# Feed-forward products of steps 3 to 10 written turned, the conditioning rows moved behind both down products, and three weight rests cut in halves

## The reference, cut to what matters

```
def swiglu(x, w_gate_up, w_down):
    g, u = jnp.split(x @ w_gate_up, 2, axis=-1)
    return (jax.nn.silu(g) * u) @ w_down
...
        x = layer_norm(ALPHA * x + mixed, ln1_g[i], ln1_b[i])
        x = layer_norm(ALPHA * x + swiglu(x, w_gate_up[i], w_down[i]), ln2_g[i], ln2_b[i])
...
def hybrid_layer(x, c_act, norm_g, w_ada, b_ada, w_in, w_out, pos):
    mod = c_act @ w_ada + b_ada
    shift, scale, gate = jnp.split(mod, 3, axis=-1)
    h = rms_norm(x, norm_g) * (1.0 + scale[:, None, :]) + shift[:, None, :]
```

## Time and profile before

| | |
|---|---|
| median of three runs | 1551.9 us |
| the profiled execution's own time | 1551.6 us |
| span of its trace | 1549.8 us |
| PE busy | 1527.2 us of the span (99%) |
| DVE busy | 1090.6 us (70%) |
| ACT busy | 759.4 us (49%) |
| mean granted clock of PE | 0.999 of full speed |

### The profile page before, as it was taken

One profiled execution on the slowest core, in us unless ns is written; L12 is line 12 of the kernel. 1 busy time (PEld: TensorE's weight loads), 2 busy tenths in 40 slices (PEclk: granted clock), 3 DMA queues, 4 the chain that ended last, 5 costly groups with the idle time before them and its releaser, 6 DMA issues.

```text
span 1549.8 us, 19849 instructions
## 1 busy us (share of the span) xinstructions
PE 1527.2 (99%) x8091; PEld 1267.2 (82%) x8091; DVE 1090.6 (70%) x1568; ACT 759.4 (49%) x960; POOL 52.8 (3%) x89
## 2 busy tenths in 40 slices
PE   9999999999999999999999999999999999999997
PEld 7887788888878888888788888877888888978986
DVE  6986866656787775677866757888667678567764
ACT  5657444444445443447544433566344434574463
POOL 1100000000000000000000000000100000000010
PEclk9999999999999999999999999999999999999999
DMA  8662566644435766353476654533766646433530
GB/s 323 243 227 83 207 221 263 250 172 181 163 109 193 262 260 250 136 215 112 158 258 226 245 233 143 197 109 137 272 253 240 222 164 224 164 119 140 218 123 27
DMA packets 45898, 299.87 MB, mean 193 GB/s; under 512 B 5540, under 2 KB 5796, under 8 KB 12528
## 3 DMA queue, kind: packets, MB, share of 16 engines
q1 hardware_dynamic: 39600, 278.74, 48.6%
q0 software_dynamic: 5776, 19.01, 3.7%
q10 hardware_dynamic: 432, 0.85, 0.1%
HBM read 296.20 MB, written 2.65 MB: 193 GB/s over the span
## 4 chain that ended last, share of the span: by engine, by line
PE 86%; DVE 8%; ACT 3%; issue 2%; DMA 0%; SPq 0%; POOL 0%; POOLq 0%; DVEq 0%; ACTq 0%
PE psum L1311 55%; PE psum L1270 15%; PE psum L1305 7%; DVE w_low L1779 2%; PE psum L1165 2%; PE psum L1240 1%; PE psum L1424 1%; PE psum L1327 1%; PE psum L1378 1%; PE psum L1308 1%; DVE work L2101 1%; ACT w_high L1530 1%; PE psum L1412 1%; DVE work L2063 1%; DVE w_low L1786 0%
## 5 line engine op out<-in xcount | busy, mean ns | idle before, releaser
L1530 ACT ACTIVATE w_high<-w_raw 128x2048 fp32r<-128x2048 f32 (+1 forms) x240 | 456.3, 1903 | 230.1 <-DMA w_raw<-in_weights 144.6
L1779 DVE TENSOR_TENSOR w_low<-w_raw,w_high 128x2048 fp32r<-128x2048 f32 (+2 forms) x240 | 526.0, 2196 | 40.2 <-ACT w_high L1530 39.2
L1311 PE MATMUL psum<-w_high,xt_high 128*128 128x512 f32 (+1 forms) x1376 | 378.6, 395 | 1.3 <-ACT xt_high L1539 1.3
L1311 PE MATMUL psum<-w_high,xt_low 128*128 128x512 f32 (+1 forms) x1376 | 368.4, 388 | 0.3 <-DVE xt_low L1813 0.3
L1311 PE MATMUL psum<-w_low,xt_high 128*128 128x512 f32 (+1 forms) x1376 | 368.1, 388 | 0.0
L1311 PEld LDWEIGHTS psum<-w_high,xt_low 128*128 128x128 f32 x1376 | 257.4, 188 | 54.8 <-DVE xt_low L1813 0.7
L1311 PEld LDWEIGHTS psum<-w_low,xt_high 128*128 128x128 f32 x1376 | 257.3, 188 | 54.0 <-DVE w_low L1765 0.5
L1311 PEld LDWEIGHTS psum<-w_high,xt_high 128*128 128x128 f32 x1376 | 249.8, 188 | 52.1 <-ACT xt_high L1539 1.8
L2130 DVE TENSOR_TENSOR arena<-arena,psum 128x256 f32<-128x256 f32 x88 | 37.0, 420 | 203.5 <-ACT arena L1665 203.1
L1665 ACT ACTIVATE arena<-psum 128x256 f32<-128x256 f32 x88 | 33.7, 383 | 217.7 <-PE psum L1311 217.7
L1270 PE MATMUL psum<-w_high,ht_high 128*128 128x512 f32 x352 | 99.9, 401 | 0.0
(11 more groups left out here) (253 smaller groups left out, 1498.5 us busy)
## 6 DMA issues: line engine op xcount, KB each, us to landing
w_raw<-in_weights SPq DMA_DIRECT2D x260, 1024.0 KB, 4.8
norm_params<-in_ln_g POOLq DMA_DIRECT2D x8, 512.0 KB, 4.2
norm_params<-in_ln_b POOLq DMA_DIRECT2D x8, 512.0 KB, 5.9
w_raw<-in_weights SPq DMA_DIRECT2D x4, 656.0 KB, 6.4
kv_outside<-arena POOLq DMA_DIRECT2D x3, 512.0 KB, 5.8
mem_kv<-kv_outside POOLq DMA_DIRECT2D x3, 512.0 KB, 3.5
norm_params<-mods_outside POOLq DMA_DIRECT2D x3, 512.0 KB, 5.9
x_rows<-in_x SPq DMA_DIRECT2D x4, 256.0 KB, 5.6
```

The costliest lines, as they stand in the source:

```text
L1311: m = e.matmul(psum[:, bank, 0:w], rows[:, kk, rb * P:rb * P + P], right[:, at:at + w], start=first, stop=last)
L1530: e.activation(K.w_hi[:, g % RING, 0:w], K.w_raw[:, r, 0:w], ACT.Copy).then_inc(K.high.hit(t), 1)
L1779: m = e.tensor_tensor(K.w_lo[:, s, 0:n], K.w_raw[:, r, 0:n], K.w_hi[:, s, 0:n].bitcast(F32), ALU.subtract)
```

## The change

- **Blocks of steps 3 to 10** (`BY_ROWS = 3`) become `block_up`: now 128 columns of weights stand still and x streams. `w_high` meets both parts of x in one matmul of 512 columns (256 of `xt_high`, 256 of `xt_low`, two stretches of the new tile `xt_both`), and `w_low` meets the high part alone in a matmul of 256 columns. A block is 32 matmuls of 512 and 32 of 256 columns. Its result is already turned, so `turn_h` with its transposes is gone for these eight steps.
- **Banks.** The two halves of a block (n = 0 and n = 1) each need two banks at once: n = 0 takes both of `gemms`, n = 1 takes both of `tr`.
- **ACT and DVE.** The two halves of a bank have to be added up. For each n, ACT copies the second halves of both banks to SBUF (`ff_rest`), DVE adds the first halves to them (two instructions, which free the banks), ACT makes silu, and DVE multiplies. Then ACT and DVE split h from SBUF (`split_h`).
- **Down products** stand two steps behind their block and no longer three; that of step 6 is spread over the steps 8 and 9.
- **The conditioning row** (`ada_row`) now stands behind both calls of the down product.
- **Halves.** The rest of a weight tile that would stand right ahead of an `rms` is cut in two, with `rms` between the halves. The plan finds three such places.

```diff
-BOTH = ("turned", "memory", "tail", "queries")
+BOTH = ("turned", "memory", "tail", "queries", "up")
...
+    def block_up(self, layer, step, gen):
+        uses = [(ring.take(), ring.take()) for ring in (self.gemms, self.tr)]
+        for half in range(2):
+            t = self.tile("w_gate_up", layer, step, "up", 4 * half)
+            for n in range(2):
+                self.gemm(t, n, half, gen, ("gemm", "turn")[n], uses[n], "up")
+                if half:
+                    self.add("gate_turned", Up(layer, step, n, uses[n], t))
+                    if n:
+                        self.add("split_h", (layer, step))
+                self.on()
...
-            self.block("w_gate_up", layer, step, gen, gate(step), "up")
-            self.ada_row()
+                self.block("w_gate_up", layer, step, gen, gate(step), "up")
+            else:
+                self.block_up(layer, step, gen)
...
+            for rb in range(RB) if step < FF_STEPS - 3 else (step - FF_STEPS + 3,):
+                down(min(step - 2, FF_STEPS - 5), t, rb)
+                if rb:
+                    self.ada_row()
+                self.on()
+                if rb == 0 and step == BY_ROWS - 1:
+                    turn(step)
...
-            if what == "scores":
+            if what in ("scores", "rms"):
                 self.rest_halves[n] = t
...
+    def gemm_up(j, hi, lo):
+        ring = (K.gemms, K.tr)[j.rb]
+        if j.half == 0:
+            for use in j.use:
+                pe.wait_ge(*ring.free(use))
+        banks = [psum[:, ring.place(use), :] for use in j.use]
...
+        for kk, b, c in work:
+            e.matmul(banks[b].rearrange("p (n s) -> p n s", n=2), hi[:, c:c + P], K.xt_both[:, :, kk, :], start=kk == 0, stop=False)
+        pe.wait_ge(*K.taken.at(j.tile))
+        for kk, b, c in work:
+            m = e.matmul(banks[b][:, 0:SEQ], lo[:, c:c + P], K.xt_both[:, 0, kk, :], start=False, stop=kk == KC - 1)
...
+    def gate_turned(j):
+        ring = (K.gemms, K.tr)[j.n]
+        first = min(ring.place(use) for use in j.uses)
+        act.wait_ge(*K.multiplied.at((j.tile, j.n)))
+        if j.step > BY_ROWS:
+            act.wait_ge(*K.h_made.at((j.layer, j.step - 1, j.n)))
+        e.activation(K.ff_rest[j.n], psum[:, first:first + 2, SEQ:BLK], ACT.Copy).then_inc(K.rest_out.hit((j.layer, j.step, j.n)), 1)
+        act.wait_ge(*ring.out(j.uses[0]))
+        e.activation(K.ff_silu[j.step % 2][:, j.n, :], K.ff_gate(j), ACT.Silu).then_inc(K.silu_done.hit((j.layer, j.step, j.n)), 1)
...
+        v.wait_ge(*K.rest_out.at((j.layer, j.step, j.n)))
+        for use, row in zip(j.uses, (K.ff_gate(j), K.ff_up(j))):
+            e.tensor_tensor(row, psum[:, ring.place(use), 0:SEQ], row, ALU.add).then_inc(ring.sem(use), 1)
...
+        e.tensor_tensor(K.ff_h[j.step % 2][:, j.n, :], K.ff_silu[j.step % 2][:, j.n, :], K.ff_up(j),
+                        ALU.mult).then_inc(K.h_made.hit((j.layer, j.step, j.n)), 1)
```

More of the change, by code:

```diff
@@ L145 @@
 Ff = namedtuple("Ff", "layer step rb use tile")
+Up = namedtuple("Up", "layer step n uses tile")
 Ada = namedtuple("Ada", "row use")
@@ L1248, in idle @@
             e.matmul(psum[:, K.wide.place(0), :], K.zeros[:, 0:P], K.zeros[:, :], start=True, stop=True)
+    def gemm_up(j, hi, lo):
[4 more added lines that the diff above has]
+        banks = [psum[:, ring.place(use), :] for use in j.use]
+        for r in range(RB):
+            use = plan.xt_uses[j.gen, r, j.half]
+            pe.wait_ge(*K.xt_high.at(use))
+            pe.wait_ge(*K.tr.out(use))
+        work = [(4 * j.half + k, b, k * BLK + b * FF_STEP + j.rb * P) for k in range(4) for b in range(2)]
+        pe.wait_ge(*K.high.at(j.tile))
+        for kk, b, c in work:
[3 more added lines that the diff above has]
+            m = e.matmul(banks[b][:, 0:SEQ], lo[:, c:c + P], K.xt_both[:, 0, kk, :], start=False, stop=kk == KC - 1)
+        m.then_inc(K.multiplied.hit((j.tile, j.rb)), 1)
     def gemm(j):
@@ L1252, in gemm @@
         hi, lo = K.w_hi[:, s, :], K.w_lo[:, s, :]
+        if j.kind == "up":
+            gemm_up(j, hi, lo)
+            return
         if j.kind == "down":
@@ L1263, in gemm @@
                 elif n == 1:
-                    pe.wait_ge(*K.tr.out(plan.ff_turn[j.gen[1], j.half]))
+                    pe.wait_ge(*(K.tr.out(plan.ff_turn[j.gen[1], j.half]) if j.half < BY_ROWS
+                                 else K.ht_low.at((j.gen[1], j.half))))
                 else:
@@ L1675, in turn_h, with split_h @@
                      ACT.Copy).then_inc(K.ht_high.hit(j), 1)
+    def gate_turned(j):
[7 more added lines that the diff above has]
+        e.activation(K.ff_silu[j.step % 2][:, j.n, :], K.ff_gate(j), ACT.Silu).then_inc(K.silu_done.hit((j.layer, j.step, j.n)), 1)
+    def split_h(j):
+        layer, step = j
+        if step > 3:
+            act.wait_ge(*K.multiplied.at((plan.down_tile[layer, step - 4], 1)))
+        for n in range(2):
+            act.wait_ge(*K.h_made.at((layer, step, n)))
+        e.activation(K.ht_hi[step % 4], K.ff_h[step % 2], ACT.Copy).then_inc(K.ht_high.hit(j), 1)
     def ada_halves(row):
@@ L2541, in __init__ @@
         self.ada_acc = ff[12:14]
+        self.ff_rest = [work[:, BLK * n:BLK * n + BLK].rearrange("p (b s) -> p b s", b=2) for n in range(2)]
         self.prob = [work[:, 1024 * n:1024 * n + 1024] for n in range(2)]
@@ L2737, in group_on_scalar, with ff_gate, ff_up @@
         return 0 if by_rows(j) and self.unit_pieces(j) > 4 else None
+    def ff_gate(self, j):
+        places = [(self.gemms, self.tr)[j.n].place(use) for use in j.uses]
+        return self.ff_rest[j.n][:, int(places[0] > places[1]), :]
+    def ff_up(self, j):
+        places = [(self.gemms, self.tr)[j.n].place(use) for use in j.uses]
+        return self.ff_rest[j.n][:, int(places[0] < places[1]), :]
     def unit_pieces(self, j):
```

44 lines of the change are left out of this document (28 added, 16 removed).

## The result

The changed kernel takes 1577.8 us in the median of 4 runs (1577.38 to 1578.55), against 1551.7 us for the kernel before, measured beside it: a ratio of 1.0164, 95% interval 1.0152 to 1.0176 (the quotient of the two medians is 1.0168). The profiled execution took 1577.4 us, its span is 25.8 us longer than before.

What follows compares the result with a forecast made beforehand. PE, busy 1527.2 of 1549.8 us, was taken to set the time; -14.7 + 6.7 - 0.5 us on PE and +17.3 us of new waits made +8.8 us, so 1560.7 us, range 1548 to 1569 us.

Steps and rivals of the forecast that it cites:

- Transposes and turned blocks: On PE in 32 blocks of steps 3 to 10: transposes gone -14.7 us, turned blocks +6.7 us.
- Two stretches in the stream: On PE, 512-column matmuls that stream two stretches of SBUF: zero extra taken, upper bound 13.6 us.
- Waits for the bank: PE in steps 6 and 8 waits for DVE's row reading: 8 places, 2.5 and 1.9 us, +17.3 us.
- The loop: Buffer loop over DVE, transfer and ACT takes 17.1 us against a 16.5 us step, so DVE falls back 0.6 us.
- Halves: Rests split around the norms of the last layers: -0.5 us at the second norm, 0 at the other two places.
- The step that failed: In the sum: PE's waits in steps 6 and 8, 4.3 us in a layer, 8 places, counted as +17.3 us.
- the third rival: Same as "More than forecast": dearer transfer or two-stretch stream, up to +13 us on top, 1574 us; chance 0.15.
- No new wait: DVE reads the conditioning row's bank before PE needs it at S+19.75; only -8.5 us remains, 1543.4 us; chance 0.13.
- the wait, but no backlog: PE waits for the row's bank without DVE falling back: 8 x 1.3 = 10.4 us, 1553.8 us; chance 0.22.
- More than forecast: Transfer takes longer or the streamed pair of stretches costs: +3 to +13 us on top, 1564 to 1574 us; chance 0.15.

Runs made afterwards that it cites:

- Experiment 6: The changed kernel with DVE's split of h moved behind the `low` that follows a block: 1552.5 us in one run.
- experiment 2: The changed kernel with useless 512-column matmuls on PE ahead of the blocks of steps 6 (12) and 8 (8): 1568.3 us, ratio 1.0099.
- experiments 1: The changed kernel with the conditioning row between the two calls of the down product: 1552.8 us, ratio 1.0001 to the kernel before.
- experiment 7: The changed kernel with `ada_sum` behind the row in steps 5 and 7, and DVE's split of h behind the `low`: 1546.0 us, ratio 0.9957.
- experiment 4: The changed kernel with the conditioning row right behind the block, ahead of the down product, as in the kernel before: 1585.8 us in one run.

## Why the prediction was right or wrong

The forecast was 1560.7 us with a range up to 1569; it came out at 1577.8. Slower was right, and so was the mechanism of the waits; what follows on a wait was missing. Its steps one by one:

- **Transposes and turned blocks: right, a little too hopeful.** -0.46 and +0.21 us a step were forecast, -0.25 in sum; measured is -0.20. A block takes 11.15 us, not 11.1: a group of 512 columns that follows on one of 256 takes 1.84 us (237.83 to 239.67) where the first in a block takes 1.82 or 1.81. In 32 steps that is 1.6 us.
- **Two stretches in the stream: right.** Eight such matmuls take 1.81 us (268.75 to 270.56), which is 8 x 0.227, the price of matmuls with one stretch. The upper bound of 13.6 us was empty.
- **Waits for the bank: right in place, count and order, near in size.** Eight of them, on the first 512-column group of n = 1 in steps 6 and 8. Forecast 2.5 and 1.9 us; measured 2.70 to 3.14 and 1.86 to 1.98, in total 19.5 instead of 17.3 (4.3 us in a layer make 17.2). The hand-made schedule had the `low` at S+15.0, 15.6, 16.2 and in step 7 at S+15.6; the trace has it at S+15.15, 15.86, 16.47 and 15.62, and the bank is read at S+22.55, not at S+22.2. That the waits in step 6 get longer from layer to layer was not forecast, and no run tells why.
- **The loop: right.** Experiment 6 shortens it, the `low` no longer falls back, and the waits of steps 6 and 8 become equal but for one.
- **Halves: too large alone, and wrong in the whole.** -0.5 us was forecast; alone they give -0.3, and in the changed kernel the waits of that line are 0.5 us longer than before.
- **The step that failed** is "That wait sets the loop back; step 6 has 15.0, step 7 15.6, and PE waits 1.9 us. 4.3 us in a layer": with the sum's "+17.3 us of new waits" it turns each microsecond of wait into one microsecond of time. No term and no bound of the sum was for what PE does after a wait. No wait of the kernel before is longer than 1.7 us, so none of its rows had such a case, and for want of a row its cost should have been bounded, as the other unknown costs were. The steps show 12.3 us for it, 10.5 of them from the low clock; experiment 2 shows these by themselves, and experiments 1, 6 and 7, whose new waits are at most 1.4 us, have no low clock in the layers. With the 10.5 us, the forecast would have been 1571.2 us. The rest of 6.6 us is made of longer waits (2.2), getting back to pace (1.8), blocks (1.6) and norms (1.0); less 0.5 us at the program's start, 0.5 us stay open.
- **The range** failed for the same reason: 28 us was the bound for the waits, but the range was cut at 1569 for the third rival's dearest part, and the clock stood in no case.
- **The rivals.** "No new wait" is refuted by the trace, "the wait, but no backlog" by experiment 6, where that case is made on purpose. Its waits are 0.65 us each, less than that rival's 1.3, since the split's wait for ACT has gone with it. "More than forecast" comes nearest with 1564 to 1574 us, still 4 us short, and for the wrong reasons: neither the transfer nor the two stretches cost anything of that kind.

## What to carry to other kernels

Before a reader of a PSUM bank is moved behind other work, lay out one step of the reading engine by hand and compare when it gets to the bank with when PE needs it; put the cheap reader ahead of long work that nobody waits for. Here that order and a shorter loop together (experiment 7) made the same change 0.43% faster than the kernel before instead of 1.64% slower.

Look at whether a loop over a buffer (free it, load it, convert it) is longer than a step, even by 0.6 us: each turn adds to the wait, and moving one short instruction, with its own wait, out of the loop took the waits from 19.5 to 5.2 us.

When a change makes an engine that is busy all the time wait for some 2 us or more, don't count the wait alone: here 19.5 us of waits cost 31.8.

## What the runs showed of the hardware

In the layers the granted clock of TensorE fell to its lower level, 1.2 GHz, only around waits of PE: in the changed kernel from 0.85 us before PE's restart to 1.5 us after it, in experiment 4 from 0.5 us before to 1.1 us after. A stretch (3.5 us at 0.51) cost some 1.55 us by the lengths of the steps. In these two kernels it came with all eight waits of 2.7 us or more, and with four of the eight between 1.86 and 2.22 us, without order by length: 1.86, 1.92, 2.13 and 2.16 had it, 1.93, 1.98, 2.15 and 2.22 not. Behind waits of up to 1.7 us no trace has it. What decides in the middle is open; no run was made on it. Nor is it sure that shorter waits are always safe: in 4 of the 34 executions of the kernel before that stand beside the experiments the mean clock is 0.997, less than in any trace without such a stretch, and they took 1553.1 to 1554.7 us; where their clock was low is not on record.
